# Products nobody reads in TensorE's waits at the ends of three stages of a hybrid block followed by a mixture of experts

## What is computed

```python
def rwkv7_recurrence(r, decay, k, v, kk, a):
    def step(state, inp):
        r_t, w_t, k_t, v_t, kk_t, a_t = inp
        sa = jnp.einsum('bhij,bhj->bhi', state, -kk_t)
        state = (state * w_t[:, :, None, :] + sa[..., :, None] * (kk_t * a_t)[..., None, :]
                 + v_t[..., :, None] * k_t[..., None, :])
        return state, jnp.einsum('bhij,bhj->bhi', state, r_t)
...
        mix = jnp.concatenate([mla_o, rwkv_o], axis=-1) @ w_o[i]
        x = layer_norm(DEEPNORM_ALPHA * x + (1.0 + gt1) * mix, ln1_g[i], ln1_b[i])
        h = x * (1.0 + sc2) + sh2
        ffn = moe_ffn(h, router_w[i], router_b[i], exp_w1[i], exp_b1[i], exp_w2[i], exp_b2[i])
...
def moe_ffn(h, router_w, router_b, w1, b1, w2, b2):
    logits = (ht @ router_w + router_b).astype(jnp.float32)
    top_val, top_idx = lax.top_k(logits, TOP_K)
    gates = jax.nn.softmax(top_val, axis=-1)
    # tokens are sorted by expert into blocks of 128 slots; each block: swiglu(h @ w1[e] + b1[e]) @ w2[e] + b2[e]
```

## Time and profile before

| | |
|---|---|
| median of 3 runs | 2002.92 us (2000.81 to 2012.78) |
| the profiled execution's own time | 2002.25 us |
| its span, from first to last instruction | 2000.6 us |
| TensorE busy, records | 1882.6 us (94%), 9331 |
| weight loads busy | 1502.8 us (75%) |
| VectorE busy | 1577.3 us (79%) |
| ScalarE busy | 1212.9 us (61%) |
| GpSimd busy | 437.6 us (22%) |
| mean granted clock of TensorE | 0.967 |
| line with the most time in the chain that ended last | L3394 on TensorE, 53% of the span |

### The profile page before, as it was taken

How to read it: one execution, slowest core, us unless ns; L and a number is a source line. 1 busy time by engine, 2 the same in 40 slices (tenths; PEclk the granted TensorE clock), 3 DMA queues, 4 the chain that set the end, 5 groups by cost and what they waited for, 6 DMA issues and landing times.

```text
span 2000.6 us, 27086 instructions
## 1 busy us (share of the span) xinstructions
PE 1882.6 (94%) x9331; PEld 1502.8 (75%) x9331; DVE 1577.3 (79%) x1614; ACT 1212.9 (61%) x1246; POOL 437.6 (22%) x381
## 2 busy tenths in 40 slices
PE   6989988887999797899999999999999999999997
PEld 5766655685777686788888888888888888888884
DVE  5763344684457569889999999999999999999996
ACT  5544545423455332367777777777777777777773
POOL 4435534002034242151111111111111111111110
PEclk9989988998999898799999999999999999999999
DMA  7535442405101123699999999999999999999994
GB/s 203 167 100 187 146 137 74 171 1 137 53 1 22 32 87 119 226 312 359 390 398 394 395 398 386 395 385 396 382 393 396 384 394 379 399 388 393 389 374 157
DMA packets 180401, 525.06 MB, mean 262 GB/s; under 512 B 34530, under 2 KB 52018, under 8 KB 180338
## 3 DMA queue, kind: packets, MB, share of 16 engines
q1 hardware_dynamic: 156882, 458.27, 60.4%
q0 software_dynamic: 21376, 65.95, 11.5%
q10 hardware_dynamic: 2080, 0.01, 0.1%
HBM read 499.06 MB, written 25.12 MB: 262 GB/s over the span
## 4 chain that ended last, share of the span: by engine, by line
PE 57%; DVE 1%; issue 0%; ACT 0%; POOLq 0%; POOL 0%; DVEq 0%
PE banks L3394 53%; PE banks L3382 3%; PE banks L3458 1%; PE banks L3388 1%; DVE expert_weights L3732 0%; DVE x_tokens L3728 0%; DVE x_tokens L3739 0%; PE banks L3515 0%; PE banks L3479 0%; PE banks L3449 0%; DVE u_lo L3564 0%; DVE x_tokens L3611 0%; DVE member L3591 0%; DVE route_work L3588 0%; PE banks L3447 0%
## 5 line engine op out<-in xcount | busy, mean ns | idle before, releaser
L3528 DVE TENSOR_TENSOR weights_lo<-expert_weights,weights_hi 128x2048 fp32r<-128x2048 f32 x384 | 876.2, 2288 | 66.2 <-ACT weights_hi L3768 62.3
L3768 ACT ACTIVATE weights_hi<-expert_weights 128x2048 fp32r<-128x2048 f32 x384 | 738.9, 1926 | 263.2 <-PE banks L3394 238.3
L3394 PE MATMUL banks<-weights_hi,rows_hi 128*128 128x512 f32 x1024 | 319.3, 393 | 0.0
L3394 PE MATMUL banks<-weights_hi,rows_lo 128*128 128x512 f32 x1024 | 315.6, 389 | 0.0
L3394 PE MATMUL banks<-weights_lo,rows_hi 128*128 128x512 f32 x1024 | 273.8, 389 | 0.0
L3394 PEld LDWEIGHTS banks<-weights_hi,rows_hi 128*128 128x128 f32 x1024 | 189.8, 188 | 44.9 <-issue 7.2
L3394 PEld LDWEIGHTS banks<-weights_hi,rows_lo 128*128 128x128 f32 x1024 | 192.3, 188 | 40.4
L3394 PEld LDWEIGHTS banks<-weights_lo,rows_hi 128*128 128x128 f32 x1024 | 192.2, 188 | 39.9
L3394 PE MATMUL banks<-weights_hi,u_hi 128*128 128x512 f32 x512 | 160.9, 396 | 1.3 <-DVE u_lo L3564 1.3
L3394 PE MATMUL banks<-weights_hi,u_lo 128*128 128x512 f32 x512 | 158.0, 390 | 0.0
L3394 PE MATMUL banks<-weights_lo,u_hi 128*128 128x512 f32 x512 | 137.0, 389 | 0.0
(11 more groups left out here) (602 smaller groups left out, 2800.4 us busy)
## 6 DMA issues: line engine op xcount, KB each, us to landing
expert_weights<-in_exp_w SPq DMA_DIRECT2D x384, 1024.0 KB, 10.3
enter_rows<-in_ada_w POOLq DMA_DIRECT2D x24, 1024.0 KB, 5.7
w_in_landing<-in_w_in SPq DMA_DIRECT2D x16, 384.0 KB, 3.3
second_landing<-in_w_in SPq DMA_DIRECT2D x12, 512.0 KB, 3.6
x_tokens<-in_x SPq DMA_DIRECT2D x8, 512.0 KB, 6.4
w_in_landing<-in_w_in SPq DMA_DIRECT2D x8, 512.0 KB, 3.6
rwkv_room<-in_w_o SPq DMA_DIRECT2D x8, 512.0 KB, 7.9
w_in_landing<-in_w_in SPq DMA_DIRECT2D x12, 256.0 KB, 4.2
```

The lines of the kernel that those rows point to most:

```text
L3394: last = nc.tensor.matmul(c.banks[:, bank + n, :], left[:, 2 * q + kk, :], right[:, q, kk * FF + n * 512:kk * FF + (n + 1) * 512], start=s ...
L3528: nc.vector.tensor_tensor(w_lo[:, ch % SPLIT, :], c.raw[:, ch % RAW if place is None else place, :], w_hi[:, ch % SPLIT, :], ALU.subtract) ...
L3768: nc.scalar.activation(w_hi[:, ch % SPLIT, :], c.raw[:, ch % RAW if place is None else place, :], ACT.Copy).then_inc(hi_ready.sem, 1)
```

## The change

Three stretches of products are added whose results nobody reads.

```diff
@@ joined, TensorE, behind the last logits of the "leave" block
                     turn_h(3)
                     logits(3)
+                    pe.wait_ge(taken.sem, 2 * TT)
+                    for _ in range(10):
+                        nc.tensor.matmul(c.banks[:, 0, :], yT[:, 0, 0, 0:P], yT[:, 0, 0, :], start=True, stop=True)
@@ rwkv_core, TensorE, ahead of the wait for the block inverses
+                def idle(bank, n):
+
+                    for _ in range(n):
+                        nc.tensor.matmul(c.banks[:, bank, :], c.ident[:], v_tok[:, 0, :], start=True, stop=True)
+
+                idle(0, 3)
                 pe.wait_ge(solved.sem, 1)
@@ rwkv_core, TensorE, behind the last outputs
                 outputs(TT - 1)
+                idle(0, 10)
@@ experts, TensorE, ahead of count_members
+                for _ in range(4):
+                    nc.tensor.matmul(c.banks[:, 2, :], c.ident[:], h[:, 0, 0:512], start=True, stop=True)
                 count_members()
                 turn_gates()
                 first_rows(0, turned_bank)
```

## The result

The changed kernel takes 2007.92 us (median of 22 runs, 2004.07 to 2018.19), against 2004.53 (22 runs of the kernel before, 1997.21 to 2012.78). The ratio is 1.0030, 95% interval 1.0019 to 1.0041, so 3.8 to 8.2 us slower. It is slower, as forecast, and inside the range, and the cost at the block's end came by the mechanism named. But the forecast's size, +3.7 us or 0.18%, lies under the interval: the sum counted nothing behind the routing, and something was lost there. The profiled execution of the changed kernel took 2005.70 us (span 2004.0) against 2002.25 (span 2000.6).

The account below looks back on a forecast made before the run. TensorE bounds the expert loop at 34.98 us per expert, passing on earlier gains or losses. Terms: +0.7 before the solving loop, -0.6 at rwkv_core's end, +4.2 at the block's end, -0.6 in routing: +3.7, forecast 2006.5 us, range 2002.0 to 2010.5.

Parts of the forecast that it names:

- the cost at the block's end: Behind the last logits: TensorE arrives last, so ten added products make all engines enter the experts 4.2 us later.
- as I had doubted: In the routing: doubted that TensorE stays at full clock to the gathering, since counting uses narrow products; sum unaffected.

Follow-up runs that it names:

- D alone: The kernel before with only four products added at the start of the experts, ahead of count_members: 2006.28 us, ratio 1.0032.
- twenty at C: The kernel before with only twenty one-pass products added behind the last logits: 2008.53 us, ratio 1.0028.
- both with ten at B: The kernel before with only ten products added at the end of rwkv_core, timed twice: 2008.59 us, ratio 1.0033, and 2002.17 us, ratio 0.9996.

## What to carry to other kernels

An engine that idles at a stage's end is free to use only if it is not the last one to arrive there: ten products in front of a block's end cost their full 3.9 us, and the same work behind it delays nothing up to the loop. The mean clock is no measure of a gain: here it rose, and the kernel became slower. Before filling a wait to raise the clock, ask what each faster product is waited for by, and where the half-clock time goes instead: a gap widened on TensorE is paid for by the products behind it. And for effects of 0.2%, time the unchanged kernel under another name beside the rest, and read the stages of more than one profile of it.

## What had not been expected of the hardware

- The clock can fall behind a gap as well as in it: in D alone it was 1.00 in 844 to 848 us, with 0.29 us of work in four, and 0.57 in 848 to 850, with TensorE busy for all of it. In the second trace of the same kernel it fell at 843.1, within the gap of 4.40 us. The Trainium skill, page "TensorE: Matmul & The Clock Gate", section "Part 1: The HAM clock gate (the "warmup" mystery)", ties the half clock to an engine that has not been busy lately. The trace agrees, and adds where the price falls either way: on the dense products behind.
- Full clock was lost within one gathering and regained in it: in the changed kernel at 835.4, 0.3 us after the products had begun behind an idle time of 1.02, until 838.8. Four and ten dense products shortly before had not kept it up, as I had doubted.
- The same program meets its half-clock stretches at other places in each execution: between `solved` and the output block the unchanged kernel took 71.01 and 69.59 us. Stages in which TensorE is not what others wait for (the routing, 20.54 to 20.88 in the ten traces without products at D) hardly show it.
- 1.2 to 1.6 us without anything that the profile shows precede TensorE's first products behind the loop when 68, 88 or 108 records (products and weight loads) are added ahead of it; with 20 or fewer and with 256 there is no such time. With 40 (twenty at C, and both with ten at B) the bias products themselves end 0.5 to 1.0 us later. What it is is open.
